# A one-layer diffusion step on one core: four modulation pieces ahead of the input projection instead of six, and their bias added on VectorE

## The chip, the core and the metric

The kernel runs on one NeuronCore of a Trainium2 chip. Its engines are PE (TensorE, matrix products), ACT (ScalarE), DVE (VectorE), POOL (GpSimd) and SP (SyncE, which here only issues DMAs). Time is device microseconds of one execution, and lower is better. Before the change three runs gave a median of 1856.68 us (1853.46 to 1857.34).

## What is computed

One layer over 640 tokens of width 1024: 128 context tokens (block 0) and 512 latent tokens (blocks 1 to 4). The part that the change touches:

```python
def modulation(cond, w_mod, b_mod):
    m = jax.nn.silu(cond) @ w_mod + b_mod          # (1024) @ (1024, 6144), for c and for c_ctx
    return jnp.split(m[..., None, :], 6, axis=-1)
...
sh1, sc1, g1, sh2, sc2, g2 = modulation(c, w_mod[l], b_mod[l])
h = rmsnorm(xs, norm1_g[l]) * (1 + sc1) + sh1
q, k, v, f = split_in(h, w_in[l])                  # h @ w_in, (1024, 2048)
...
xs = xs + g1 * mixer_merge(att, four, subln_g[l], lam_init, w_out[l])
h2 = rmsnorm(xs, norm2_g[l]) * (1 + sc2) + sh2
xs = xs + g2 * peer(h2, w_query[l], sub_keys[l], expert_u[l], expert_v[l])
```

Only shift 1 and scale 1 (the first third of the modulation) are needed by `h`, which the input projection takes; the rest is needed after the attention. Then follow rotary embedding, differential attention, a Fourier mix, an output projection, and a product-key retrieval over 16384 experts, in a loop of 64 passes that takes most of the time.

## The kernel before

Everything is float32. The kernel is written engine by engine in program order, with semaphores between engines; each engine runs its own list in order.

**Weights.** `w_mod` comes in 12 pieces of 1024x512 (2 MiB each, mod 0 to mod 11), `w_in` in four of the same size, which the code calls k, q, v and f by the heads that they give. All of them, then a table for the Fourier mix and two pieces of `w_out`, go through a ring of three slots of 2 MiB (`chunk`, `WRING = 3`). SP issues the loads in one order, `chunk_order()`: mod 0 to 5, k, mod 6, mod 7, q, mod 8, mod 9, v, mod 10, mod 11, f. Ahead of load i SP waits until piece i-3 has been used (L353). PE counts that in `s_chunk_used`: after the last product of a modulation piece, and after an input piece's last block (L1382, where PE first waits for its own last product and then runs a nop). SP is in order, so a load that has to wait holds back every later load.

**A modulation piece.** Both conditions at once: the 32-column array tiles hold (condition, half of the columns) in four groups of rows 0, 32, 64, 96, and PE runs 32 products of 256 columns (L1328), then four of one row times the bias (L1337), into one of eight PSUM banks. `mod_out(j)` on ACT copies row groups to `rows` (a ring of two, L557), and `spread_mod` on POOL broadcasts each of the four rows over 128 partitions (L451), into `M1` for mod 0 to 3 and into `M` or `G2` for the others.

**From the first four pieces to the projection.** DVE waits for 16 broadcasts (mod 0 to 3), turns scale 1 into (1 + scale) times the norm's weight (L873, two instructions of 1024 columns), and makes `H1` block by block in two instructions (L880, L882). PE transposes a block (L1354), ACT rounds it into `HT_hi` (L586), and DVE keeps the rest in `HT_lo` (L928). The piece of `w_in` is split in the same way, `w_hi` on ACT (L580, `weights_high`) and `w_lo` on DVE (L920, `weights_low`), each in eight steps. DVE's order is: three blocks of H1, `rows_low(0)`, half of `weights_low(0)`, `rows_low(1)`, the other half.

**The projection.** For each of k, q, v, f and each of five blocks PE runs 8 times three products of 512 columns (L1372, L1373, L1376); of block 0 each step waits for its `w_lo`. Blocks of k and q are rotated on DVE (L906 to L913), transposed back on PE (`headT`, L1389) and copied by ACT (L567). Between the input pieces PE computes the modulation pieces that `mods_ahead` names, two each time. I call the stretch from the last block of one input piece to the first product of the next a gap: gap 1 before q, gap 2 before v, gap 3 before f.

The order in which PE fills the eight banks is `_phase1_jobs()`; entry n needs that entry n-8 was emptied.

Of the kernel before, what the change touches and what calls it, by code (L numbers as in the profile page):

```python
# [20 lines left out]
MOD_FIRST = 6  # L21
# [30 lines left out]
def mods_ahead(ci):  # L52

    return [MOD_FIRST + 2 * (ci - 1) + w for w in range(2)]

# [10 lines left out]
def _phase1_jobs():  # L66
    jobs = [(("mod", j), "act") for j in range(MOD_FIRST)]
# [4 lines left out]
    for ci, (c, turned) in enumerate((("k", None), ("q", "k"), ("v", "q"), ("f", None))):  # L72
        if ci:
            jobs += [(("mod", j), "act") for j in mods_ahead(ci)]
# [52 lines left out]
def program(nc, xall, condT, w_mod, b_mod, norm1_g, w_in, lam4, subln_g, w_fourier, w_out, norm2_g,  # L127
# [7 lines left out]
    with ctx:  # L135
        def sb(name, shape, dt=f32):
            return ctx.enter_context(nc.sbuf_tensor(name, shape, dt))
# [5 lines left out]
        ones = sb("ones", [1, 32])  # L143
# [111 lines left out]
        bmod = cutout(CO, 6144, slice(0, 1))  # L255
        gbc = creg[:, 6144:8192].rearrange("p (w d) -> p w d", w=2)
        rows = creg[:, 8704:9216].rearrange("p (r n) -> p r n", r=2)
        bmod_late = cutout(XO + 4096, 1024, slice(0, 1))
# [31 lines left out]
        s_chunk_used = sem("s_chunk_used")  # L290
# [5 lines left out]
        s_rows = sem("s_rows"); s_bc = sem("s_bc")  # L296
# [36 lines left out]

        block = ctx.enter_context(nc.Block())
# [100 lines left out]
        def _(pool):  # L435
# [5 lines left out]
            def spread_mod(j):  # L441
                pool.wait_ge(s_rows, j + 1)
# [82 lines left out]
        def _(act):  # L525
            act.dma_start(cond[:, :, :], condT).then_inc(s_cond, 16)
            act.dma_start(bmod, b_mod).then_inc(s_bmod, 16)
# [7 lines left out]
            act.wait_ge(s_set, 1)  # L535
# [16 lines left out]

            def mod_out(j):
                src = bank1("mod", j)
                if j >= 2:
                    act.wait_ge(s_bc, 4 * (j - 1))
                act.copy(rows[:, j % 2, :], src[:, 0:HC]).then_inc(s_rows, 1)  # L557
                act.wait_ge(s_rows, j + 1)
                act.nop().then_inc(s_act1, 1)

            for j in range(MOD_FIRST):
                mod_out(j)

# [31 lines left out]
            def between(ci):  # L595

                mod_out(mods_ahead(ci)[0])
                weights_high(ci)
                mod_out(mods_ahead(ci)[1])

            for ci, c in enumerate(("k", "q")):
                if ci:
                    between(1)
                for b in range(NBLK):
# [8 lines left out]
                    else:  # L613
                        dst = kT if c == "k" else qT
# [8 lines left out]
            between(2)  # L623
            act.dma_start(bmod_late, b_mod[:, 10 * NC:12 * NC]).then_inc(s_bmod, 16)
# [9 lines left out]
            between(3)  # L634
# [206 lines left out]
        def _(dve):  # L841
# [11 lines left out]
            dve.memset(ones[:, :], 1.0).then_inc(s_set, 1)  # L853
# [15 lines left out]
            dve.tensor_scalar(ss[:, :], ss[:, :], 1.0 / D, EPS, ALU.mult, ALU.add).then_inc(s_var1, 1)  # L869
            dve.wait_ge(s_bc, 16)  # L870
# [12 lines left out]

            def bank1(*name):
                i = B1.pos[name]
                dve.wait_ge(s_fill1, i + 1)
                return ps[:, i % 8, :]
# [53 lines left out]
            for ci, c in enumerate(("k", "q")):  # L941
                for b in range(1, NBLK):
# [10 lines left out]
            dve.nop().then_inc(s_mod2, 1)  # L953
            weights_low(3)
            dve.tensor_copy(fold[:, 1], bank1("fold", 1).rearrange("p (g n) -> p g n", g=4)).then_inc(s_dve1, 1)
# [351 lines left out]
        def _(pe):  # L1307
# [12 lines left out]
            pe.wait_ge(s_set, 1)  # L1320
            pe.wait_ge(s_bmod, 16)
            def modulation(j):
# [3 lines left out]
                for k in range(KD):  # L1326
                    for q in range(4):
                        last = nc.tensor.matmul(out[32 * q:32 * q + 32, 0:HC], sil[:, k, q % 2, :],  # L1328
                                                chunk[:, i % WRING, k, q // 2 * HC:(q // 2 + 1) * HC],
                                                start=(k == 0), stop=False)  # L1330
                last.then_inc(s_chunk_used, 1)
                if j >= 8:
                    pe.wait_ge(s_bmod, 32 if j < 10 else 48)
                for q in range(4):
# [385 lines left out]
```

## Time and profile before

| what | value |
|---|---|
| median of 3 runs (lowest, highest) | 1856.68 us (1853.46, 1857.34) |
| span of the profiled execution | 1849.2 us |
| PE busy, of the span | 1726.7 us (93%) |
| DVE busy | 1498.4 us (81%) |
| POOL busy | 898.5 us (49%) |
| ACT busy | 678.4 us (37%) |
| HBM traffic over the span | 281 GB/s |
| modulation and projection (first product to last block of f) | 12 to 206 us |

The profiled execution's own time is given as its span alone, from its first instruction to its last, 7.5 us under the median of the runs. Busy shares are means over stages that have different limits: the expert loop, from about 440 us to the end, keeps PE, DVE and the DMA engines busy together, while the change lies in the first 206 us. There the question is at each point which of the engines or loads ended last.

### The profile page before, as it was taken

To read this page: it belongs to the slowest core of one execution; us is meant where nothing else is said; L and a number is where in the kernel's file an instruction comes from. 1 tells how busy PE (TensorE), PEld (TensorE's weight loads), DVE (VectorE), ACT (ScalarE), POOL (GpSimd) and SP (SyncE) were. 2 spreads that over 40 slices of the span, in tenths; PEclk is the share of its full clock that TensorE was granted. 3 is DMA by queue.
4 is the path that set the end of the run, shared out by engine and by line. 5 is a ranking of instruction groups with operands and counts; after the bars stand their busy time and mean duration, and the time that the engine had idled before them with its cause. 6 is when DMAs were issued, how large, how long until landed. Compare 5 with 4: busy or idle time off the path is not lost.

```text
span 1849.2 us, 29905 instructions
## 1 busy us (share of the span) xinstructions
PE 1726.7 (93%) x9942; PEld 1481.5 (80%) x9942; DVE 1498.4 (81%) x3027; ACT 678.4 (37%) x1135; POOL 898.5 (49%) x742
## 2 busy tenths in 40 slices
PE   4999998989899997699999999999999999999994
PEld 2677657448788886699999999999999999999993
DVE  0732057237888979899999999999999999999997
ACT  1212147010667763233333333333333333333332
POOL 1111001000242433488887878888666666666661
PEclk8999989999999998799999999999999999999997
DMA  9455101610055646899999999999999999999993
GB/s 355 163 186 223 62 1 42 243 46 1 2 110 114 134 101 183 314 402 399 405 401 392 403 407 407 403 404 401 407 405 396 403 407 399 398 405 407 402 397 138
DMA packets 253543, 520.91 MB, mean 282 GB/s; under 512 B 113955, under 2 KB 130979, under 8 KB 252197
## 3 DMA queue, kind: packets, MB, share of 16 engines
q1 hardware_dynamic: 178016, 249.00, 37.9%
q0 software_dynamic: 73728, 268.47, 36.7%
q10 hardware_dynamic: 1734, 2.60, 0.4%
q8 instruction: 38, 0.62, 0.1%
q14 instruction: 27, 0.22, 0.0%
HBM read 488.55 MB, written 31.46 MB: 281 GB/s over the span
## 4 chain that ended last, share of the span: by engine, by line
PE 57%; DVE 23%; issue 12%; DMA 5%; ACT 2%; DVEq 1%; SPq 0%; POOL 0%; POOLq 0%; PEldq 0%; ACTq 0%
DVE arena L1243 12%; PE ps L1626 9%; PE ps L1625 9%; PE ps L1624 9%; PE ps L1541 6%; PE ps L1522 4%; PE ps L1595 4%; DMA arena_w<-in_w_mod 2%; PE ps L1372 2%; PE ps L1376 2%; PE ps L1373 2%; PE ps L1459 2%; PE ps L1420 1%; DMA arena_w<-in_w_in 1%; DVE C_lo L1218 1%
## 5 line engine op out<-in xcount | busy, mean ns | idle before, releaser
L1624 PE MATMUL ps<-hT_hi,U_hi 128*128 128x384 f32 x1024 | 344.7, 337 | 11.7 <-DVE U_lo L1188 11.7
L1626 PE MATMUL ps<-hT_hi,U_lo 128*128 128x384 f32 x1024 | 344.7, 337 | 0.0
L1625 PE MATMUL ps<-hT_lo,U_hi 128*128 128x384 f32 x1024 | 344.0, 336 | 0.0
L1624 PE MATMUL ps<-V_hi,C_hi 128*128 128x512 f32 x768 | 300.1, 391 | 17.4 <-DVE C_lo L1218 17.4
L1626 PE MATMUL ps<-V_hi,C_lo 128*128 128x512 f32 x768 | 302.3, 394 | 0.0
L1625 PE MATMUL ps<-V_lo,C_hi 128*128 128x512 f32 x768 | 302.1, 393 | 0.0
L774 ACT CAST V_hi<-V_in 128x1024 fp32r<-128x1024 f32 x128 | 135.1, 1055 | 247.8 <-PE ps L1626 201.7
L480 POOL DMA_INDIRECT arena<-in_expert_u,idxn x128 | 173.4, 1355 | 81.3 <-issue 32.1
L811 ACT ACTIVATE act_t<-ps 128x384 f32<-128x384 f32 x128 | 63.0, 492 | 394.7 <-PE ps L1626 363.8
L1624 PEld LDWEIGHTS ps<-hT_hi,U_hi 128*128 128x128 f32 x1024 | 193.1, 189 | 16.8 <-issue 11.9
L480 POOL DMA_INDIRECT arena<-in_expert_v,idxn x128 | 159.0, 1243 | 93.3 <-DVE arena L1243 42.7
L1625 PEld LDWEIGHTS ps<-hT_lo,U_hi 128*128 128x128 f32 x1024 | 193.0, 189 | 4.9
L500 POOL TENSOR_SCALAR arena<-iota,arena 128x128 f32<-128x128 f32 x96 | 92.1, 970 | 208.7 <-PE ps L1595 128.9
L1626 PEld LDWEIGHTS ps<-hT_hi,U_lo 128*128 128x128 f32 x1024 | 192.9, 188 | 0.0
L1624 PEld LDWEIGHTS ps<-V_hi,C_hi 128*128 128x128 f32 x768 | 144.9, 189 | 45.5 <-DVE C_lo L1218 18.1
L1626 PEld LDWEIGHTS ps<-V_hi,C_lo 128*128 128x128 f32 x768 | 144.7, 188 | 30.7
L1243 DVE SCALAR_TENSOR_TENSOR arena<-arena,dots 128x1024 f32<-128x1024 f32 x128 | 165.0, 1289 | 4.7
L1625 PEld LDWEIGHTS ps<-V_lo,C_hi 128*128 128x128 f32 x768 | 144.8, 189 | 27.9
L1193 DVE TENSOR_TENSOR V_lo<-V_in,V_hi 128x1024 fp32r<-128x1024 f32 x128 | 156.5, 1223 | 12.9 <-ACT V_hi L774 11.5
L1188 DVE TENSOR_TENSOR U_lo<-U_in,U_hi 128x1024 fp32r<-128x1024 f32 x128 | 156.1, 1220 | 0.5 <-ACT U_hi L767 0.2
L1232 DVE SCALAR_TENSOR_TENSOR arena<-arena 128x1024 f32<-128x1024 f32 x128 | 153.7, 1220 | 3.0 <-DMA arena<-h_scratch 3.0
L767 ACT CAST U_hi<-U_in 128x1024 fp32r<-128x1024 f32 x128 | 134.0, 1047 | 34.0 <-DMA U_in<-in_expert_uT 31.6
(239 smaller groups left out, 3233.0 us busy)
## 6 DMA issues: line engine op xcount, KB each, us to landing
U_in<-in_expert_uT SPq DMA_DIRECT2D x128, 512.0 KB
V_in<-in_expert_v SPq DMA_DIRECT2D x128, 512.0 KB
arena_w<-in_w_mod SPq DMA_DIRECT2D x12, 2048.0 KB, 12.5
gates_scratch<-arena_w SPq DMA_DIRECT2D x6, 4096.0 KB, 20.8
gate_in<-gates_scratch SPq DMA_DIRECT2D x128, 192.0 KB
arena_w<-in_w_in SPq DMA_DIRECT2D x4, 2048.0 KB, 8.6
arena_w<-in_w_query SPq DMA_DIRECT2D x1, 7168.0 KB, 20.4
arena_w<-in_w_out SPq DMA_DIRECT2D x2, 2048.0 KB, 10.3
```

Of the source, the lines that this page charges most:

```text
L480: pool.indirect_dma_start(out=rowr[row], out_offset=None, in_=table, in_offset=bass.IndirectOffsetOnAxis(ap=idxn[:, g, row:row + 1], axis= ...
L500: ins = pool.tensor_scalar(rhs1[AIDED][:, t, :], iota[:, :], selT[:, b % 2, 0, at:at + 1], selT[:, b % 2, 1, at:at + 1], ALU.is_equal, ALU ...
L767: act.copy(U_hi[:, r], U_in[:, r]).then_inc(s_uhi, 1)
L774: act.copy(V_hi[:, r], V_in[:, r]).then_inc(s_vhi, 1)
L1188: dve.tensor_tensor(U_lo[:, r], U_in[:, r], U_hi[:, r].bitcast(f32), ALU.subtract).then_inc(s_ulo, 1)
L1193: dve.tensor_tensor(V_lo[:, r], V_in[:, r], V_hi[:, r].bitcast(f32), ALU.subtract).then_inc(s_vlo, 1)
L1232: dve.scalar_tensor_tensor(out=rowr[q], in0=rowr[q], scalar=1.0, in1=h2row[k], op0=ALU.mult, op1=ALU.mult, accum_out=dst).then_inc(s_used, 1)
L1243: dve.scalar_tensor_tensor(out=accS[:, k], in0=rowr[q], scalar=c, in1=accS[:, k], op0=ALU.mult, op1=ALU.add).then_inc(s_used, 1)
L1541: last = nc.tensor.matmul(out[:, j * P:(j + 1) * P], wq[:, k, c:c + P] if k < 7 else wq7[:, c:c + P], h2T[:, k, b * P:(b + 1) * P], start= ...
L1624: nc.tensor.matmul(out, hi, rhi, start=start, stop=False)
L1625: nc.tensor.matmul(out, hi, rlo, start=False, stop=False)
L1626: return nc.tensor.matmul(out, lo, rhi, start=False, stop=stop)
```

## The change

1. `MOD_FIRST` goes from 6 to 4, and `mods_ahead` gives three, three and two pieces to the gaps instead of two each. The order of loads becomes mod 0 to 3, k, mod 4, 5, 6, q, mod 7, 8, 9, v, mod 10, 11, f.
2. The bias is no longer four products on PE. It is loaded into rows 0, 32, 64 and 96 of two zeroed buffers, and `mod_out` is now one addition on DVE from the bank to `rows`.
3. `mod_out` stands on DVE: the first four after the variance of the input, and in each gap one ahead of `weights_low` and the others behind it. ACT's copies fall away.
4. SP waits on `s_fill1`, the count of filled banks, instead of `s_chunk_used`; PE's wait for itself and the nop fall away.
5. On ACT the four bias loads stand behind DVE's memset; the late bias waits for a second memset, on DVE behind the rotation of k's block 4. In q, ACT's copy of the first transposed block waits until mod 7 has been added, since the early bias lies where `qT` goes.

```diff
-MOD_FIRST = 6
+MOD_FIRST = 4
+MOD_EARLY = 8
...
 def mods_ahead(ci):
-    return [MOD_FIRST + 2 * (ci - 1) + w for w in range(2)]
+    return {1: [4, 5, 6], 2: [7, 8, 9], 3: [10, 11]}[ci]
...
-    jobs = [(("mod", j), "act") for j in range(MOD_FIRST)]
+    jobs = [(("mod", j), "dve") for j in range(MOD_FIRST)]
...
+        def bias_of(q, first, end):
+            return (b_mod.rearrange("o (j z n) -> o j z n", z=2, n=HC)[:, first:end, q // 2, :])
...
 # SP
                 if i >= WRING:
-                    sp.wait_ge(s_chunk_used, i - WRING + 1)
+                    kind, at = list(CHUNK)[i - WRING]
+                    sp.wait_ge(s_fill1, B1.pos[("mod", at) if kind == "mod" else ("z", "kqvf"[at], NBLK - 1)] + 1)
...
 # POOL
-                pool.wait_ge(s_rows, j + 1)
+                pool.wait_ge(s_dve1, B1.emptied(B1.pos["mod", j])[1])
...
 # ACT
-            act.dma_start(bmod, b_mod).then_inc(s_bmod, 16)
+            act.wait_ge(s_set, 1)
+            for q in range(4):
+                act.dma_start(bmod[32 * q:32 * q + 1], bias_of(q, 0, MOD_EARLY)).then_inc(s_bmod, 16)
...
-                mod_out(mods_ahead(ci)[0])
-                weights_high(ci)
-                mod_out(mods_ahead(ci)[1])
...
                     else:
+                        if ci and b == 1:
+                            act.wait_ge(s_dve1, B1.emptied(B1.pos["mod", MOD_EARLY - 1])[1])
...
                         if ci == 0 and b + 2 == NBLK:
-                            act.dma_start(bmod_late, b_mod[:, 8 * NC:10 * NC]).then_inc(s_bmod, 16)
+                            act.wait_ge(s_latefill, 1)
+                            for q in range(4):
+                                act.dma_start(bmod_late[32 * q:32 * q + 1], bias_of(q, MOD_EARLY, MOD_CH)).then_inc(s_bmod, 16)
...
 # DVE
-            dve.memset(ones[:, :], 1.0).then_inc(s_set, 1)
+            dve.memset(creg[:, 3072:3072 + MOD_EARLY * HC], 0.0).then_inc(s_set, 1)
...
+            def mod_out(j):
+                src = bank1("mod", j)
+                dve.wait_ge(s_bmod, 64 if j < MOD_EARLY else 128)
+                if j >= 2:
+                    dve.wait_ge(s_bc, 4 * (j - 1))
+                bias = bmod[:, j, :] if j < MOD_EARLY else bmod_late[:, j - MOD_EARLY, :]
+                dve.tensor_tensor(rows[:, j % 2, :], src[:, 0:HC], bias, ALU.add).then_inc(s_dve1, 1)
+            for j in range(MOD_FIRST):
+                mod_out(j)
             dve.wait_ge(s_bc, 16)
...
+                    if ci == 0 and b + 1 == NBLK:
+                        dve.wait_ge(s_fill1, B1.pos[("hT", NBLK - 1, 1)] + 1)
+                        dve.memset(cutout(XO + 4096, (MOD_CH - MOD_EARLY) * HC), 0.0).then_inc(s_latefill, 1)
+                mod_out(mods_ahead(ci + 1)[0])
                 weights_low(ci + 1)
+                for j in mods_ahead(ci + 1)[1:]:
+                    mod_out(j)
...
 # PE
-                last.then_inc(s_chunk_used, 1)
-                for q in range(4):
-                    at = q // 2 * HC
-                    bias = bmod[:, j * NC + at:j * NC + at + HC] if j < 8 else bmod_late[:, j % 2 * NC + at:j % 2 * NC + at + HC]
-                    last = nc.tensor.matmul(out[32 * q:32 * q + 32, 0:HC], ones[:, :], bias, start=False, stop=True)
                 last.then_inc(s_fill1, 1)
...
-                if b == NBLK - 1:
-                    pe.wait_ge(s_fill1, B1.pos[("z", c, b)] + 1)
-                    pe.nop().then_inc(s_chunk_used, 1)
```

SP, the loads from mod 0 to f (each 128x8x512 is one piece of 2 MiB; in_w_mod is modulation, in_w_in projection), before:

```order
L353 DMA arena_w<-in_w_mod 128x8x512
L341 DMA arena<-in_xall 128x5x1024
L353 DMA arena_w<-in_w_mod 128x8x512 x2
L353 DMA arena_w<-in_w_mod 128x8x512 [waits s_chunk_used] x3
L353 DMA arena_w<-in_w_in 128x8x512 [waits s_chunk_used]
L353 DMA arena_w<-in_w_mod 128x8x512 [waits s_chunk_used] x2
L353 DMA arena_w<-in_w_in 128x8x512 [waits s_chunk_used]
```

The same place of the changed kernel:

```order
L357 DMA arena_w<-in_w_mod 128x8x512
L344 DMA arena<-in_xall 128x5x1024
L357 DMA arena_w<-in_w_mod 128x8x512 x2
L357 DMA arena_w<-in_w_mod 128x8x512 [waits s_fill1]
L357 DMA arena_w<-in_w_in 128x8x512 [waits s_fill1]
L357 DMA arena_w<-in_w_mod 128x8x512 [waits s_fill1] x3
L357 DMA arena_w<-in_w_in 128x8x512 [waits s_fill1]
```

The load of k moved from seventh to fifth place, and three loads of modulation, not two, now stand between it and the load of q.

PE in gap 1 (L1389 is the last `headT` of k, L1328 and L1337 a modulation piece, L1372 q's first product; s_chunk0 to s_chunk2 are the slots of the ring), before:

```order
L1389 MATMUL ps<-ident,arena_w 128x128 [waits s_fill1,s_dve1]
L1389 MATMUL ps<-ident,arena_w 128x128 x3
L1328 MATMUL ps<-arena_w 32x256 [waits s_chunk1,s_dve1]
L1328 MATMUL ps<-arena_w 32x256 x31
L1337 MATMUL ps<-arena_w,ones 32x256 x4
L1328 MATMUL ps<-arena_w 32x256 [waits s_chunk2,s_act1]
L1372 MATMUL ps<-w_hi_next,HT_hi 128x512 [waits s_dve1,s_wlo,s_chunk0]
```

And in the changed kernel:

```order
L1386 MATMUL ps<-ident,arena_w 128x128 [waits s_dve1]
L1386 MATMUL ps<-ident,arena_w 128x128 x3
L1336 MATMUL ps<-arena_w 32x256 [waits s_chunk2,s_dve1]
L1336 MATMUL ps<-arena_w 32x256 x31
L1336 MATMUL ps<-arena_w 32x256 [waits s_chunk0,s_act1]
L1336 MATMUL ps<-arena_w 32x256 [waits s_chunk1,s_dve1]
L1373 MATMUL ps<-w_hi_next,HT_hi 128x512 [waits s_dve1,s_wlo,s_chunk2]
```

Three pieces stand here now. The third takes slot 1, where k lies until its last block, and q takes slot 2, where the first of the three lies.

DVE between the rotation of k's block 4 and that of q's block 1, before:

```order
L913 TENSOR_TENSOR arena_w<-arena_w 128x512 [waits s_step]
L920 TENSOR_TENSOR w_lo<-arena_w,w_hi_next 128x512 [waits s_whi] x8
L906 TENSOR_TENSOR arena_w<-ps,arena_w 128x512 [waits s_dve1,s_fill1]
```

And in the changed kernel:

```order
L914 TENSOR_TENSOR arena_w<-arena_w 128x512 [waits s_step]
L951 MEMSET arena 128x1024 [waits s_fill1]
L872 TENSOR_TENSOR arena_w<-ps,arena_w 128x256 [waits s_bc,s_bmod,s_fill1]
L921 TENSOR_TENSOR w_lo<-arena_w,w_hi_next 128x512 [waits s_whi] x8
L872 TENSOR_TENSOR arena_w<-ps,arena_w 128x256 [waits s_bc,s_bmod,s_fill1] x2
L907 TENSOR_TENSOR arena_w<-ps,arena_w 128x512 [waits s_dve1,s_fill1]
```

A memset and one addition now stand ahead of the split of q's weights, and two additions behind it.

## Rows read from the trace of the kernel before

**Rows 1.** The profile's page: the span, and the chain that ended last, by engine and by line.

```profile
span 1849.2 us, 29905 instructions
PE 57%; DVE 23%; issue 12%; DMA 5%; ACT 2%; DVEq 1%; SPq 0%; POOL 0%; POOLq 0%; PEldq 0%; ACTq 0%
DVE arena L1243 12%; PE ps L1626 9%; PE ps L1625 9%; PE ps L1624 9%; PE ps L1541 6%; PE ps L1522 4%; PE ps L1595 4%; DMA arena_w<-in_w_mod 2%; PE ps L1372 2%; PE ps L1376 2%; PE ps L1373 2%; PE ps L1459 2%; PE ps L1420 1%; DMA arena_w<-in_w_in 1%; DVE C_lo L1218 1%
```

**Rows 2.** The chain in order of time, front and gaps: start us, us, what.

```profile
37.54 12.53 DMA arena_w<-in_w_mod
50.11 3.66 PE ps L1328 x64
...
57.50 0.52 ACT w_hi_first L580
...
91.35 8.19 DMA arena_w<-in_w_in
99.56 0.63 ACT w_hi_next L580
...
101.05 0.47 PE ps L1372
...
130.56 8.02 DMA arena_w<-in_w_in
```

**Rows 3.** Timeline of DVE: start us, us, line, out<-in, count, [idle before <-releaser].

```profile
1.61 0.48 DVE L852 MEMSET arena_w<- 128x512 f32 x1
...
45.85 2.48 DVE L873 SCALAR_TENSOR_TENSOR arena_w<-arena_w 128x1024 f32<-128x1024 f32 x2 [18.52 <-POOL arena_w L451]
...
50.93 1.43 DVE L880 SCALAR_TENSOR_TENSOR arena<-arena,rstd,arena_w 128x1024 f32<-128x1024 f32 x1
...
55.09 1.32 DVE L882 TENSOR_TENSOR arena<-arena,arena_w 128x1024 f32<-128x1024 f32 x1
56.33 1.27 DVE L928 TENSOR_TENSOR HT_lo<-ps,HT_hi 128x512 fp32r<-128x512 f32 x2
58.04 2.50 DVE L920 TENSOR_TENSOR w_lo<-arena_w,w_hi_first 128x512 fp32r<-128x512 f32 x4 [0.43 <-ACT w_hi_first L580]
...
64.06 1.28 DVE L880 SCALAR_TENSOR_TENSOR arena<-arena,rstd,arena_w 128x1024 f32<-128x1024 f32 x1
```

**Rows 4.** Timeline of PE, front, gap 1, and after the attention.

```profile
42.88 0.63 PE L1337 MATMUL ps<-arena_w,ones 1*32 1x256 f32 x8
...
62.39 0.50 PE L1372 MATMUL ps<-w_hi_first,HT_hi 128*128 128x512 f32 x1 [0.54 <-DVE w_lo L920]
...
91.54 0.63 PE L1389 MATMUL ps<-ident,arena_w 128*128 128x128 f32 x4 [0.30 <-PE ps L1376]
...
324.21 1.12 PE L1492 MATMUL ps<-ident,arena_w 128*128 128x128 f32 x4 [4.58 <-DVE arena_w L998]
```

**Rows 5.** SP's loads of modulation in gaps 1 and 2, and their landing.

```profile
95.81 4.52 SPq L353 DMA_DIRECT2D arena_w<-in_w_mod  x2
...
DMA to landing us min/median/max: 11.4/11.4/11.4
...
135.02 4.52 SPq L353 DMA_DIRECT2D arena_w<-in_w_mod  x2
...
DMA to landing us min/median/max: 10.9/10.9/10.9
```

**Rows 6.** Two stretches: busy us of PE, PEld, DVE, ACT, POOL, PEclk, DMA, GB/s.

```profile
27.00:31.00 4.00, 4.00 (x48) 1.81 (x44) 0.17 (x1) 0.39 (x3) 1.18 (x1) 0.56 1.06 383
324.00:331.00 7.00, 6.01 (x10) 2.90 (x11) 0.16 (x1) 0.69 (x1) 0.00 (x0) 0.51 0.75 277
```

**Rows 7.** One shape of addition on DVE, one copy on ACT, PE's second modulation piece.

```profile
L909 DVE TENSOR_TENSOR arena_w<-ps,arena_w 128x256 f32<-128x256 f32 x16 | 6.0, 415 | 0.0
...
43.58 0.37 ACT L557 COPY arena_w<-ps 128x256 f32<-128x256 f32 x1 [5.10 <-PE ps L1337]
...
26.70 4.66 PE L1328 MATMUL ps<-arena_w 128*32 128x256 f32 x48 [8.12 <-DMA arena_w<-in_w_mod]
```

More of the change, by code:

```diff
@@ L73, in _phase1_jobs @@
         if ci:
-            jobs += [(("mod", j), "act") for j in mods_ahead(ci)]
+            jobs += [(("mod", j), "dve") for j in mods_ahead(ci)]
         for b in range(NBLK):
@@ L142, in program @@
         ident = sb("ident", [P, P])
-        ones = sb("ones", [1, 32])
         lam = sb("lam", [P, 8])
@@ L534, in _ @@
             act.wait_ge(s_cond, 16)
-            act.wait_ge(s_set, 1)
             act.activation(sig, cond[:, :, :], ACT.Exp, scale=-1.0).then_inc(s_exps, 1)
@@ L551, in bank1 @@
                 return ps[:, i % 8, :]
[L553 to L562, printed above, removed]
             def heads_out(name, dst):
@@ L593, in _ @@
             act.dma_start(V[:, 1, :], cache_v).then_inc(s_vc, 16)
-            def between(ci):
-                mod_out(mods_ahead(ci)[0])
-                weights_high(ci)
-                mod_out(mods_ahead(ci)[1])
             for ci, c in enumerate(("k", "q")):
                 if ci:
-                    between(1)
+                    weights_high(1)
                 for b in range(NBLK):
@@ L619, in _ @@
                         if ci == 0 and b + 2 == NBLK:
-                            act.dma_start(bmod_late, b_mod[:, 8 * NC:10 * NC]).then_inc(s_bmod, 16)
+                            act.wait_ge(s_latefill, 1)
+                            for q in range(4):
+                                act.dma_start(bmod_late[32 * q:32 * q + 1], bias_of(q, MOD_EARLY, MOD_CH)).then_inc(s_bmod, 16)
                     if b == 0 and ci:
                         heads_out(("headT", "k", NBLK - 1), kT[:, :, 5 * P:6 * P])
-            between(2)
-            act.dma_start(bmod_late, b_mod[:, 10 * NC:12 * NC]).then_inc(s_bmod, 16)
+            weights_high(2)
             for b in range(NBLK):
@@ L633, in _ @@
                     heads_out(("headT", "q", NBLK - 1), qT[:, :, 4 * P:5 * P])
-            between(3)
+            weights_high(3)
             for b in range(NBLK):
@@ L953, in _ @@
             dve.nop().then_inc(s_mod2, 1)
+            mod_out(mods_ahead(3)[0])
             weights_low(3)
+            for j in mods_ahead(3)[1:]:
+                mod_out(j)
             dve.tensor_copy(fold[:, 1], bank1("fold", 1).rearrange("p (g n) -> p g n", g=4)).then_inc(s_dve1, 1)
@@ L1329, in modulation @@
                                                 chunk[:, i % WRING, k, q // 2 * HC:(q // 2 + 1) * HC],
-                                                start=(k == 0), stop=False)
-                last.then_inc(s_chunk_used, 1)
-                if j >= 8:
-                    pe.wait_ge(s_bmod, 32 if j < 10 else 48)
-                for q in range(4):
-                    at = q // 2 * HC
-                    bias = bmod[:, j * NC + at:j * NC + at + HC] if j < 8 else bmod_late[:, j % 2 * NC + at:j % 2 * NC + at + HC]
-                    last = nc.tensor.matmul(out[32 * q:32 * q + 32, 0:HC], ones[:, :], bias, start=False, stop=True)
+                                                start=(k == 0), stop=(k == KD - 1))
                 last.then_inc(s_fill1, 1)
@@ L1439, in _ @@
             pe.wait_ge(s_fill1, B1.total)
-            pe.nop().then_inc(s_chunk_used, 1)
             pe.wait_ge(s_act1, B1.count("act"))
```

17 lines of the change are left out of this document (7 added, 10 removed).

## The prediction

> **What bounds the kernel now.** I read the page first, then the chain in order of time over the first 206 us, then the timelines of DVE, PE and SP there, and last the granted clock around PE's pauses. The page [rows 1] gives the span, 1849.2 us, and says that over the whole program modulation loads hold only 2% of the chain and projection loads 1%; the expert loop has the rest. The loop starts when the stages ahead of it are done and runs at its own rate, so a shift of its start passes to the end one to one. The stages in between are one string of PE work with nothing loaded late, so they pass a shift on too. The change is worth what it moves the first product of each of k, q, v and f.
>
> The chain there [rows 2] has two patterns. In the front it goes from a modulation load (landed at 37.54 + 12.53 = 50.07) to PE's sixth piece, then over ACT to w_hi at 57.50. In gaps 1 and 2 it goes from PE's last block to a projection load, issued at 91.35, landed at 99.54, first split step at 99.56, first product of q at 101.05; the next one is issued at 130.56 and lands at 138.58. The modulation pieces of the gap cost nothing there: they are multiplied while that load flies.
>
> But the chain shows only who came last. DVE [rows 3] begins L873 at 45.85, when the broadcasts of mod 3 end, and is then busy with H1 and HT_lo without a pause until it waits 0.43 us for w_hi and starts w_lo at 58.04. So DVE is late by nearly as much as the load: whatever leaves the front behind mod 3, k's first product cannot follow it further than DVE allows.
>
> **The front.** Mod 4 and 5 leave it, each a load of 2 MiB; at 383 GB/s [rows 6] that is 5.5 us each, 11.0 in all, and by the chain one would book that. DVE allows this:
> - Four bias products fall away. For mod 3 they are 0.63 us [rows 4], ahead of the copy, the broadcasts and L873. The copy is now an addition: 0.42 us on DVE (the same shape, L909) for 0.37 on ACT [rows 7], and ACT's nop goes. I take -0.6.
> - POOL no longer broadcasts mod 4 and 5 beside H1. L880 takes 1.43 us there and 1.28 later [rows 3]; two of them, -0.3.
> - The wait of 0.43 for w_hi goes, since the transposes no longer stand behind mod 5 on PE: -0.4.
> - So k starts at about 57.6 in place of 58.9. Its one stall of 0.54 [rows 4] goes too, as DVE leads by more: -0.5.
> - Against that, PE has almost nothing to do from 43 to 57.6. The trace shows what follows a pause: after 8.12 us of idle [rows 7] the granted clock is 0.56 over 27 to 31, that is mostly the lower level of 1.2 GHz, and 4.00 us of work there lose 4.00 x 0.44 = 1.8 us; after 4.58 us [rows 4] it is 0.51 over 324 to 331, and 6.01 busy us lose 2.9 [rows 6]. For k's start I take the row with the like pause, +1.8; bounds 0 and 2.9.
>
> The front's sum is -1.8 + 1.8 = 0.0, between -1.8 and +1.1. Next late there is DVE, then PE.
>
> The slower start is covered. DVE's memset is four times 0.48 us [rows 3], ACT's loads and its exponent come some 3 us later, but mod 0 was waiting for its load, and behind it PE idles 8.12 us for mod 1 [rows 7].
>
> **Gaps 1 and 2.** Call T the end of k's last block. Slot 1 is k's until T, so mod 6 can be issued only then, and SP, in order, issues q behind it; q also needs mod 4 done, which PE runs after T. So the projection load that was first behind T is now second, about 4.5 us later, with mod 7 third, behind mod 5. The trace has a load in exactly that place: in gap 1 SP issues modulation at 95.81 and 99.96 [rows 5], the first of these 4.46 us behind q, and it lands 11.4 us later, at 107.2. Put q there: 107.2 - 99.54 = +7.7. Gap 2: 135.02 + 10.9 = 145.9 against 138.58, +7.3. In both PE starts its first piece 0.3 us earlier, since its wait for its own product goes (the idle ahead of L1389 [rows 4]), so -0.3 each. Sum **+14.4**. Bounds: q lands 8.19 us behind its own issue as a first load does, which costs just the later issue, 4.46 - 0.3 = +4.2 a gap; or 12.53 behind it, as in the full queue of the front, 95.81 + 12.53 - 99.54 - 0.3 = +8.5 a gap [rows 2]. I take 11.4 and 10.9, the same place among the same neighbours.
>
> Why 11.4 when a load alone takes 8.2? By the row the second load ran beside the first until 99.5 and beside the third from about 101, and slowed with both. The Trainium skill, "DMA: Bandwidth & Descriptors", section on queues, rings and completion order, says that on each DMA engine the descriptors of one queue are consumed in ring order; by that a third load would not slow the second. It stands as a rival below.
>
> PE then waits. Mod 6 lands 8.2 us behind T, its products take 3.66 [rows 2], and q starts near T + 17: idle for 5.1 us. That lies by the pause of 4.58 us, which brought the lower clock [rows 4, 6]. q's products are paced by PE, so it loses 1.8 to 2.9 us; I take the mean, 2.3, in each gap: **+4.6**, bounds 0 and 5.8. The Trainium skill, "TensorE: Matmul & The Clock Gate", section on why this matters for your kernels, advises against pauses between bursts of matmuls for this reason; the sum above has it from the rows.
>
> Hidden in the gaps: DVE's memset of 1024 columns (twice 0.48) and one addition of 0.42 stand before q's w_lo, but that waits for q to land. The two additions behind w_lo stand ahead of a rotation which needs q's block 1. ACT, waiting for the late memset, holds back one headT copy; it has nothing else until q lands. In gap 2 ACT makes four copies that used to lie among q's blocks, after mod 7 is added, 4.5 us behind T; mod 8 waits about 1 us for a bank by it, but v lands at T + 15. Were v early instead, these would cost some 2 us. POOL's broadcasts of mod 4 to 11 are for uses far behind.
>
> **Gap 3** is as before: two pieces, both loaded ahead, and f is the first load behind v's last block.
>
> **Sum:** 0.0 + 14.4 + 4.6 = **+19.0 us**. The profiled execution would have a span of 1868.2. The median of the runs lies 7.5 above the span, so 1856.7 + 19.0 = **1875.7 us**, +1.0%. A measurement of this kernel can tell about 0.2%, 3.7 us, from no change.
>
> **The rivals.**
> - *The clock holds.* No product runs at 1.2 GHz, neither in the gaps nor in the front: 19.0 - 4.6 - 1.8 = +12.6, 1869.3. For it: only two pauses of this length are on record here, and neither follows a run of modulation products by 5 us. Against: both rows after pauses of over 4 us show the drop. Chance 0.13.
> - *Loads in strict order.* q lands one load behind mod 6, 99.5 + 5.5, a gap costs 5.5, the two 11.0, with the clock 15.6: 1872.3. Against it are the 11.4 and 10.9 us of [rows 5], 2 us later than this would give. Chance 0.13. This is the rule of the DMA page above.
> - *Everything late at once:* 12.5 us per second load and 2.9 of clock in all three places: 1.1 + 17.0 + 5.8 = +23.9, 1880.6. Chance 0.08.
> - *The front gives what the chain books.* k starts when its pieces are there: -11.0 for two loads, -0.6 for the bias, -0.3 for the broadcasts, -0.5 for the stall, and each gap costs only q's later issue, 4.2: -12.4 + 8.4 = -4.0, 1852.7, faster by 0.22%. It decides if DVE's work behind mod 3 can begin before 45.85 or be done in under 2 us. For it: the chain runs over DMA, PE and ACT in the front. Against it: L873 waited 18.52 us for POOL, which waits for mod 3, a load that keeps its place, and 11 us of DVE's instructions follow with no gap. Chance 0.03.
> - *The change does not act:* if SP's new waits were all met early, time would stay. The listing of SP's order shows the three loads between k and q, and the slots follow from that. Chance 0.02.
>
> **How the numbers follow.** The forecast has 0.61, and its own bounds are 1873 to 1878. The range reaches down past the held clock and up past the case with everything late: 1867 to 1882. Faster by over 0.2%: 0.03. Within 0.2%: 0.02. Slower by over 0.2%: 0.95.
>
> **What would show it.** L873 starts near 45.2 and k's first product near 57.5; if that were near 48, the front's reading is wrong. Behind T the first load is modulation and q is issued 4 us later, lands near T + 15.5, and q's first product is 7 us further from T than the 9.7 of before; the same in gap 2, while gap 3 stays as it was. The granted clock is below 1 at the start of k, q and v. From f's first product on both traces run alike. A gap near 14 us says strict order; a clock of 1.00 there says that rival. The prediction is wrong if the gaps are as long as before.

## The result, and the profile after

The changed kernel takes **1866.84 us** (median of 4 runs, 1864.51 to 1867.24), the kernel before 1856.08 (4 runs, 1853.46 to 1857.34). The ratio is 1.0059, 95% interval 1.0046 to 1.0071: slower by 10.8 us. The forecast was slower by 19.0. The sign and the place are right, the size is nearly twice too large; the result lies at the foot of the forecast's range (1867 to 1882, reckoned from a median before of 1856.68). Why is the subject of what follows.

The page of the changed kernel, as [rows 1]:

```profile
span 1862.4 us, 29705 instructions
PE 57%; DVE 21%; issue 12%; DMA 6%; ACT 2%; DVEq 1%; POOL 0%; ACTq 0%; SPq 0%; POOLq 0%
```

DMA's share of the chain went from 5 to 6%, and the span is 13.2 us longer. The chain in order of time, gaps 1, 2 and 3 (start us, us, what), beside [rows 2]:

```profile
89.94 3.63 PE ps L1336 x64
93.58 10.63 DMA arena_w<-in_w_in
104.24 0.62 ACT w_hi_next L573
104.89 0.70 DVE w_lo L921
105.73 0.47 PE ps L1373
...
139.22 11.36 DMA arena_w<-in_w_in
...
181.67 8.14 DMA arena_w<-in_w_in
```

In [rows 2] q's load was issued at 91.35, as soon as k's last block was done, and landed 8.19 us later. Now PE first multiplies mod 4 (L1336, 3.63 us), only then q's load goes out, and it takes 10.63 us; v's takes 11.36. In gap 3 f's load takes 8.14 us. In the kernel before it took longer, which [rows 2] don't show:

```profile
168.16 9.11 DMA arena_w<-in_w_in
```

DVE in the front (start us, us, line, out<-in, count, idle before), beside [rows 3]:

```profile
42.06 0.42 DVE L872 TENSOR_TENSOR arena_w<-ps,arena_w 128x256 f32<-128x256 f32 x1 [5.00 <-PE ps L1336]
44.38 2.48 DVE L879 SCALAR_TENSOR_TENSOR arena_w<-arena_w 128x1024 f32<-128x1024 f32 x2 [1.90 <-POOL arena_w L455]
...
54.27 1.28 DVE L929 TENSOR_TENSOR HT_lo<-ps,HT_hi 128x512 fp32r<-128x512 f32 x2
55.47 2.48 DVE L921 TENSOR_TENSOR w_lo<-arena_w,w_hi_first 128x512 fp32r<-128x512 f32 x4
```

DVE turns the scale 1.5 us earlier than in [rows 3] (44.38 for 45.85; the line is now L879) and is then busy up to `w_lo` without a wait. PE's waits (the same columns), beside [rows 4]:

```profile
38.33 3.66 PE L1336 MATMUL ps<-arena_w 128*32 128x256 f32 x64 [1.76 <-DMA arena_w<-in_w_mod]
...
49.50 1.97 PE L1355 MATMUL ps<-ident,arena 128*128 128x128 f32 x8 [6.92 <-DVE arena L888]
...
56.30 0.47 PE L1373 MATMUL ps<-w_hi_first,HT_hi 128*128 128x512 f32 x1 [2.63 <-DVE w_lo L921]
...
98.97 3.66 PE L1336 MATMUL ps<-arena_w 128*32 128x256 f32 x64 [1.99 <-DMA arena_w<-in_w_mod]
105.73 0.47 PE L1373 MATMUL ps<-w_hi_next,HT_hi 128*128 128x512 f32 x1 [3.10 <-DVE w_lo L921]
...
140.33 7.11 PE L1336 MATMUL ps<-arena_w 128*32 128x256 f32 x128 [1.18 <-ACT arena_w L560]
152.08 0.62 PE L1373 MATMUL ps<-w_hi_next,HT_hi 128*128 128x512 f32 x1 [4.64 <-DVE w_lo L921]
```

SP's issues in gap 1 (start us, us, queue, line, out<-in, count), modulation first and q's piece second, where [rows 5] have the second place taken by modulation:

```profile
89.53 0.37 SPq L357 DMA_DIRECT2D arena_w<-in_w_mod  x1
93.58 0.37 SPq L357 DMA_DIRECT2D arena_w<-in_w_in  x1
```

The granted clock at the starts of k, q, v and f (columns as in [rows 6]: busy us of PE, PEld, DVE, ACT, POOL, PEclk, DMA, GB/s):

```profile
57.00:61.00 4.00, 4.00 (x13) 3.14 (x12) 4.00 (x8) 1.44 (x3) 0.00 (x0) 0.61 0.00 0
105.00:110.00 5.00, 4.27 (x19) 3.58 (x20) 5.00 (x9) 3.50 (x7) 0.00 (x0) 1.00 1.04 387
152.00:157.00 5.00, 4.92 (x15) 3.94 (x16) 4.81 (x9) 2.85 (x6) 0.43 (x2) 0.66 1.05 389
191.00:196.00 5.00, 4.67 (x21) 3.90 (x22) 4.72 (x9) 3.10 (x6) 0.19 (x1) 1.00 0.98 404
```

The clock is partly at the lower level at the starts of k and v, and at the full one at those of q and f. The next table is from PE's timelines of both kernels, in us. An input piece runs from the start of its first product to the end of its last one:

| | before | after | moved |
|---|---|---|---|
| k starts | 58.88 | 56.30 | -2.58 |
| k runs | 32.19 | 33.03 | +0.84 |
| gap 1 | 9.98 | 16.40 | +6.42 |
| q runs | 29.23 | 29.23 | 0.00 |
| gap 2 | 9.81 | 17.12 | +7.31 |
| v runs | 27.79 | 29.40 | +1.61 |
| gap 3 | 10.90 | 9.85 | -1.05 |
| f runs | 27.29 | 27.30 | +0.01 |
| f's last product ends | 206.07 | 218.63 | +12.56 |

Nearly everything happens up to f's last product: 12.56 of the span's 13.2 us.

### The profile page after: what moved, and what is told of

Read it like the earlier page. It is cut to its first block, busy times and chain, and to the rows that moved or that the text cites. A ratio compares the mean times of both kernels' runs of the same rounds, so it can differ in the third digit from the quotient of the medians.

```text
span 1862.4 us, 29705 instructions
## 1 busy us (share of the span) xinstructions
PE 1724.7 (93%) x9846; PEld 1485.0 (80%) x9846; DVE 1504.1 (81%) x3040; ACT 677.1 (36%) x1123; POOL 892.9 (48%) x742
## 4 chain that ended last, share of the span: by engine, by line
PE 57%; DVE 21%; issue 12%; DMA 6%; ACT 2%; DVEq 1%; POOL 0%; ACTq 0%; SPq 0%; POOLq 0%
PE ps L1622 9%; PE ps L1621 9%; PE ps L1620 9%; DVE arena L1253 9%; PE ps L1537 6%; PE ps L1518 4%; PE ps L1591 4%; DMA U_in<-in_expert_uT 3%; DVE V_lo L1203 3%; PE ps L1373 2%; PE ps L1377 2%; PE ps L1374 2%; DMA arena_w<-in_w_in 2%; PE ps L1455 2%; PE ps L1417 1%
## 5 line engine op out<-in xcount | busy, mean ns | idle before, releaser
L484 POOL DMA_INDIRECT arena<-in_expert_u,idxn x128 | 168.2, 1314 | 81.3 <-issue 32.1
```

What stands on the lines that cost most here:

```text
L484: pool.indirect_dma_start(out=rowr[row], out_offset=None, in_=table, in_offset=bass.IndirectOffsetOnAxis(ap=idxn[:, g, row:row + 1], axis= ...
```

## The experiments

Each ratio is against runs of the kernel before that were made beside the experiment: 17 for e1 to e4 (median 1855.04 us), 22 for e4b, e6, e7 and e8 (1855.3), 15 for e9 (1854.63), 10 for e9b (1854.46) and 15 for e10 (1855.33). `arena_w` is the buffer region that holds the loads, `bank1(...)` the PSUM bank of a named result.

### One half of the change at a time

**e1_bias_dve**: pieces as before (6, 2, 2, 2), bias added on DVE.

```diff
-MOD_FIRST = 4
+MOD_FIRST = 6
...
-    return {1: [4, 5, 6], 2: [7, 8, 9], 3: [10, 11]}[ci]
+    return [MOD_FIRST + 2 * (ci - 1) + w for w in range(2)]
...
-            for j in range(MOD_FIRST):
+            for j in range(4):
...
+            for j in range(4, MOD_FIRST):
+                mod_out(j)
```

> The changed kernel with the pieces placed as before (six first, then two in each gap); the bias on DVE stays, and mod 4 and 5 are added behind the third block of H1. If the place of the pieces costs the time, nothing of the +10.8 us is left: between -3 and 0 us against the kernel before, from mod 3 being broadcast 1 to 1.5 us sooner and PE's wait for its own product gone. If the additions on DVE or the later loads on ACT cost it, +5 us or more stays.

**e2_order_only**: the kernel before with four pieces first and three, three and two in the gaps, bias still on PE.

```diff
-MOD_FIRST = 6
+MOD_FIRST = 4
...
-    return [MOD_FIRST + 2 * (ci - 1) + w for w in range(2)]
+    return {1: [4, 5, 6], 2: [7, 8, 9], 3: [10, 11]}[ci]
...
+        bmod_mid = cutout(MO + 3072, 2048, slice(0, 1))
...
```

> The kernel before with the pieces placed as in the change (4, 3, 3, 2), bias still as products on PE and copies on ACT. If the place of the pieces is the cause: +11 to +16 us against before, a little more than the change itself, since each piece keeps its 0.63 us of bias products and the front is not helped. If DVE's additions are the cause: within 3 us of before.

Measured: e1 1854.4 us, ratio 0.9997 (0.9988 to 1.0006); e2 1869.66 us, ratio 1.0071 (1.0058 to 1.0084). The bias on DVE alone is worth nothing that can be measured, and the order alone brings the whole loss. Gaps 1, 2 and 3 are 11.35, 9.56 and 9.89 us in e1 and 16.73, 16.14 and 11.39 in e2. That e2 is above the changed kernel, by ratio 0.0012 with overlapping intervals, leaves open whether the bias gives something back in the new order.

### What makes the second load late

**e3_hold**: the changed kernel, but SP holds the load behind a projection load until that one has landed. If the load behind q takes bandwidth from q, this must shorten the gap. The table of the Fourier stage is held behind f in the same way.

```diff
+                if 0 < i < DFT_C and list(CHUNK)[i - 1][0] == "in":
+                    sp.wait_ge(s_chunk[(i - 1) % WRING], 16 * ((i - 1) // WRING + 1))
...
+                    sp.wait_ge(s_chunk[i % WRING], 16 * (i // WRING + 1))
```

> The changed kernel, but SP issues no further load until the projection piece in flight (k, q, v, f) has landed. If loads in flight share the DMA engines: q and v land about 9 us behind their issue instead of 10.6 and 11.4, f 1 us sooner or at the same time, together -3 to -5 us against the changed kernel, so +6 to +8 against before. If loads of one queue are served in order: q and v land as now, +10.8 against before within 1 us.

Measured: 1868.85 us, ratio 1.0071 (1.0056 to 1.0086). The chain of e3_hold in order of time, and in the second fence SP's issues in gap 1:

```profile
93.81 10.33 DMA arena_w<-in_w_in
...
140.49 10.50 DMA arena_w<-in_w_in
```

```profile
93.81 0.37 SPq L359 DMA_DIRECT2D arena_w<-in_w_in  x1
104.16 32.64 SPq L359 DMA_DIRECT2D arena_w<-in_w_mod  x3
```

The third load now goes out at 104.16, when q has landed, and q still takes 10.33 us in place of 10.63, v 10.50 in place of 11.36. The gaps are 16.10, 16.27 and 9.93 us, so 0.3 and 0.9 us came back where sharing would have given some 2 us each, and in the whole time nothing did. My reason in the prediction falls as the main one. Whether the third load costs v anything isn't settled: e7_five below has it and lands v after 10.71.

What is left is the load ahead. In gap 1 of the changed kernel q lands 5.4 us behind mod 6 (mod 6 was there at 98.8, q at 104.2), which is one load of 2 MiB at 383 GB/s [rows 6]. That looks as if the queue handed over one load after the other. The Trainium skill, "DMA: Bandwidth & Descriptors", section on queues, rings and completion order, states that each DMA engine takes the descriptors of a ring in order; the two landings in gap 1 agree with it. As a price it is too low in general: in gap 2 v lands 7.5 us behind mod 9 (143.1 and 150.6), in gap 2 of e3_hold it is 6.5 us, and in the kernel before the second loads of [rows 5] land 7.7 and 7.3 us behind the first. Counted from the issue of the first load the second is steadier: 14.3 to 15.9 us in all of these gaps, where it is issued 4.0 to 4.5 us behind the first. Why it is more than one load's time stays open.

**e7_five**: five pieces first, two behind k, three behind q. Gap 1 has q's load first again, gap 2 has v's load second.

```diff
-MOD_FIRST = 4
+MOD_FIRST = 5
...
-    return {1: [4, 5, 6], 2: [7, 8, 9], 3: [10, 11]}[ci]
+    return {1: [5, 6], 2: [7, 8, 9], 3: [10, 11]}[ci]
...
```

> The changed kernel with five pieces first, then two, three and two. Now k's load has q's load as the third behind it and takes its slot, so behind k's last block q is issued first; behind q's last block a modulation piece still is. If the place of the projection load in the queue decides: gap 1 about 9.8 us, gap 2 about 16 to 17, gap 3 about 10, +5 to +8 against before. If the number of pieces behind the first ones decides, each costing alike, also about half; but if three pieces in a gap were harmless and something in the front costs, +9 or more.

Measured: 1858.5 us, ratio 1.0023 (1.0014 to 1.0032). Its gaps are 10.02, 16.47 and 9.74 us. The chain of e7_five:

```profile
90.50 8.31 DMA arena_w<-in_w_in
...
133.80 10.71 DMA arena_w<-in_w_in
```

Only the gap in which a modulation load goes ahead of the projection load is long, and it is long by the same 6 to 7 us. The loss follows the place in the queue, not the number of pieces in the gap.

**e8_q_first**: the changed kernel with q, v and f each loaded first behind the last block, and the pieces that no longer fit multiplied behind the first blocks of q, v and f.

```diff
+WITHIN = {("q", 0): 6, ("v", 0): 8, ("v", 1): 9, ("f", 0): 10, ("f", 1): 11}
...
+    order = [("mod", j) for j in range(MOD_FIRST)] + [("in", 0), ("mod", 4), ("mod", 5), ("in", 1), ("mod", 6), ("mod", 7),
+             ("in", 2), ("mod", 8), ("mod", 9), ("in", 3), ("mod", 10), ("mod", 11)]
...
```

> The changed kernel with the loads in another order: k, mod 4, mod 5, q, mod 6, mod 7, v, mod 8, mod 9, f, mod 10, mod 11, so that behind each last block the projection load is issued first; mod 6 is multiplied behind q's block 0, mod 8 and 9 behind v's blocks 0 and 1, mod 10 and 11 behind f's. If q's place in the queue makes gap 1 16.4 us: it is 9.8 here, gap 2 and 3 about 9.8 too, and q's stage is 3.7 us longer, v's and f's 7.3. If DVE's additions, the memset or the late bias on ACT make it: gap 1 stays at 13 us or more. The table of the Fourier mix now waits for f's last block, so behind f some 11 us are lost, and the whole is slower than the changed kernel.

Measured: 1887.42 us in its single run, so without an interval. PE's timeline of e8_q_first at the start of the Fourier stage:

```profile
237.53 3.63 PE L1409 MATMUL ps<-arena_w 128*128 128x512 f32 x4 [8.50 <-issue]
```

q's load has the first place behind k again and lands after 9.09 us by the chain.

The gaps are 10.80, 9.62 and 9.90 us, so the place in the queue is confirmed a second time; but as a cure it fails. The pieces now cost 3.7 to 4.1 us each inside q, v and f, where nothing hides them. With fewer pieces in the gaps PE pauses for 5.42 us before v and 9.74 before f, and the granted clock is 0.52 over 144 to 149 and 0.50 over 191 to 196.5. The table for the Fourier stage, loaded last, leaves PE idle for 8.50 us behind f.

### What the clock takes

**e4_warm** and **e4b_warm**: the changed kernel with filler products of the identity in PE's pauses in the front, gap 1 and gap 2, written into the bank that is filled next. Shown is e4b; e4 has about twice as many in each pause.

```diff
+            def warm(out, count):
+                for _ in range(count):
+                    nc.tensor.matmul(out[:, 0:P], ident[:, :], ident[:, :], start=True, stop=True)
...
+            warm(bank1("hT", 0, 0), 29)
+            warm(bank1("hT", 1, 0), 3)
+            warm(bank1("z", "k", 0), 10)
...
+                if ci in (1, 2):
+                    warm(bank1("z", c, 0), {1: 11, 2: 17}[ci])
```

> The changed kernel with PE kept busy in its pauses by small products of ident with itself (58, 10 and 28 in the front, 12 and 22 in gap 1, 34 in gap 2), into banks that are filled next. If the granted clock costs what the trace shows (about 1.7 us at k's start, 1.6 at v's, none at q's in the profiled execution): clock 1.00 there and -2 to -5 us against the changed kernel, +6 to +9 against before. If products of this size do not hold the clock, or it costs nothing: +10 to +12.

> The changed kernel with PE's pauses filled again, with half as many products (29, 3 and 10 in the front, 7 and 11 in gap 1, 17 in gap 2), since one of them takes 0.223 us (58 took 12.95) and not 0.11. If the granted clock costs what the stages show (k's stage 1.4 us longer than with the clock up, v's 1.6, q's 0 to 2.8 by the execution): k and v as short as in the overfilled run (31.4 and 27.8), no stage longer, and -2 to -5 us against the changed kernel, +6 to +9 against before. If filling costs as much as it gives: +10 to +12.

e4_warm took 1877.95 us, ratio 1.0118 (1.0103 to 1.0132). PE's timeline of e4_warm:

```profile
41.86 13.12 PE L1362 MATMUL ps<-ident 128*128 128x128 f32 x116
```

58 fillers take 13.12 us, 0.226 each and not half of that (each shows as two passes), so they overran the pause of 6.92 us and pushed the work behind them. With half as many, e4b_warm took 1861.87 us, ratio 1.0034 (1.0021 to 1.0046), against 1.0059 of the changed kernel: 0.0025 of 1855 us, 4.6 us gained, or 1 to 8 with both intervals. The clock of e4b_warm, same columns as above:

```profile
56.00:60.00 4.00, 3.45 (x14) 2.59 (x15) 4.00 (x8) 1.54 (x3) 0.00 (x0) 1.00 0.00 0
104.50:109.00 4.50, 4.41 (x19) 3.67 (x20) 4.50 (x9) 2.87 (x6) 0.00 (x0) 1.00 1.04 386
150.60:155.00 4.40, 4.36 (x19) 3.64 (x20) 4.40 (x9) 2.82 (x6) 0.00 (x0) 1.00 1.03 380
```

The clock stays at its higher level at all three starts, with gaps as long as in the changed kernel (16.36, 16.79, 9.93 us). So by the medians the clock at these starts is worth nearly half of the changed kernel's loss. Not all of that need be the change's doing: the kernel before loses clock at the start of k or f in some executions too, as e10's trace shows below.

### The front

**e6_late_loads**: the kernel before, with ACT's small loads held back by a longer memset, as the changed kernel holds them back.

```diff
-            dve.memset(ones[:, :], 1.0).then_inc(s_set, 1)
+            dve.memset(ones[:, :], 1.0)
+            dve.memset(creg[:, 9216:11264], 0.0).then_inc(s_set, 1)
...
+            act.wait_ge(s_set, 1)
             act.dma_start(bmod, b_mod).then_inc(s_bmod, 16)
```

> The kernel before, where ACT issues its eight small loads behind a memset of 2048 columns on DVE, at 4.4 us instead of 1.2, as the change does. If that is why mod 3 landed 1 us sooner in the changed kernel (the DMA engines moved 164 GB/s from 8 to 10 us before and 405 after): the dip is gone, mod 5 lands about 1 us sooner, and k's first product too, 0 to -1.5 us against before. If the earlier landing had another cause: 39.3 us as before for mod 3, no difference.

Measured: 1853.42 us, ratio 0.9994 (0.9985 to 1.0003). The first large loads in the kernel before, and then in e6_late_loads:

```profile
8.00:10.00 2.00, 0.00 (x0) 0.00 (x0) 0.00 (x0) 0.00 (x0) 0.00 (x0) 1.00 0.59 164
```

```profile
8.00:10.00 2.00, 0.00 (x0) 0.00 (x0) 0.61 (x3) 1.23 (x2) 0.00 (x0) 1.00 1.02 389
```

While ACT's small loads run beside mod 0, the kernel before moves 164 GB/s; held back, it moves 389. The string of six loads then runs 0.65 us ahead (mod 3's products at 38.64 for 39.29, k's first product at 58.24 for 58.88). That is the same shift, in part, that the changed kernel has at mod 3 (38.33). In the whole time it can't be told from none.

### A version that beats both

**e9_warm_later**, **e9b_free_bank** and **e10_fill_only** are the kernel before, with its own order, and with fillers in the two pauses behind the attention, of which the first is in [rows 4, 6] (4.58 us idle, then 0.51 over 324 to 331). e9 and e9b have e6's late loads too, e10 has not. e9 puts the last 28 fillers into the bank of the third `h2T` block, e9b and e10 into a bank that is free.

```diff
+                if b == NBLK - 1:
+                    pe.wait_ge(s_exp, 2 * len(UNITS))
+                    warm(ps[:, 0, :], 17)
                 pe.wait_ge(s_att, b + 1)
...
+            warm(ps[:, 0, :], 3)
             pe.wait_ge(s_mix, NBLK)
...
+                if b == 2:
+                    warm(ps[:, 4, :], 28)
                 pe.wait_ge(s_h2, b + 1)
```

> The kernel before with its small loads delayed (as in e6_late_loads, 1853.42 us) and filler products of 0.223 us each in the two later pauses of PE that the profile shows with a low clock behind them: 17 ahead of the last attT and 3 ahead of the merge (pause 4.58 us, then 6.01 busy us at 0.51, a loss of 2.9 us), and 28 ahead of the third h2T block (pause 6.99 us, then 0.84 over 407 to 414 with 6.02 busy us, a loss of about 1.0). If the loss behind a pause is what the prediction took it for, a time that reaches the expert loop, the granted clock reads 1.00 over 324 to 331 and over 407 to 414 and the time falls by 3.9 us to about 1849.5. If the fillers end after the transposes become ready, the time stays near 1853.4. If the rest of those stages is paced by DVE or by loads, the clock rises and the time doesn't move.

> e9_warm_later with its 28 later fillers in a bank that nobody waits for. There they sat in the bank of the third h2T block and waited for ACT's copy at 406, so that they ran at half the clock behind the pause, 9.12 us, and pushed the transposes from 406.3 to 415.0; the first 20 fillers held the clock at 1.00 and won 2.5 us up to the end of the merge (from 8.3 us behind to 397.26 against 397.41 in e6_late_loads, with the first projections done 2.4 us later). If the fillers fit in the pause (28 of 0.223 are 6.2 us in 6.99), the transposes start at 406 with the clock at 1.00 over 407 to 414 and the time is 2.5 + 1.0 us under e6_late_loads' 1853.4: 1849.9. If only the earlier pause pays, 1850.9. If the expert loop doesn't take the gain, 1853.4.

> The kernel before with the 48 fillers of e9b_free_bank and nothing else, so without the delayed small loads. e9b_free_bank took 1848.7 us beside 1854.46 of before (ratio 0.9968), e6_late_loads, which has the delayed loads alone, 1853.42 beside 1855.3 (0.9994). If the two parts add up, this one has a ratio of 0.9974, some 1850 us, and nearly all the gain is the clock behind the two pauses. If the delayed loads carry a part that e6_late_loads' own interval hid, it stays above 0.9985.

| | median us | ratio | interval |
|---|---|---|---|
| e9_warm_later | 1858.21 | 1.0021 | 1.0012 to 1.0030 |
| e9b_free_bank | 1848.70 | 0.9968 | 0.9956 to 0.9980 |
| e10_fill_only | 1851.50 | 0.9978 | 0.9969 to 0.9987 |

PE's timeline of e9_warm_later:

```profile
406.07 9.12 PE L1491 MATMUL ps<-ident 128*128 128x128 f32 x56 [6.90 <-ACT arena L734]
415.04 2.78 PE L1543 MATMUL ps<-ident,arena_w 128*128 128x128 f32 x24
```

The 28 fillers wait for ACT to empty their bank, run behind the pause instead of in it, partly at the lower level of the clock, and cost 8.7 us of path. In the free bank they fill it (e9b_free_bank, PE's timeline):

```profile
400.32 6.42 PE L1491 MATMUL ps<-ident 128*128 128x128 f32 x56
407.49 3.02 PE L1543 MATMUL ps<-ident,arena_w 128*128 128x128 f32 x24 [0.75 <-ACT arena L734]
```

The chains show what either pause gave in the profiled executions. e6_late_loads comes first, then e9b_free_bank:

```profile
326.54 71.04 PE ps L1523 x160
...
406.31 2.81 PE ps L1532 x12
409.14 0.59 ACT arena L734
409.74 1.57 ACT arena L734 x3
411.31 0.25 issue
411.56 7.40 PE ps L1542 x64
```

```profile
329.81 68.95 PE ps L1532 x160
...
406.76 5.00 ACT arena L734 x10
411.76 0.24 issue
412.01 7.40 PE ps L1553 x64
```

The merge takes 68.95 us in place of 71.04, in e10's trace too. The stretch behind the second pause takes 5.25 us in both (406.31 to 411.56, 406.76 to 412.01): with a fast PE, ACT's ten copies set it. So in these executions the 20 fillers before the merge gave 2.1 us and the 28 later ones nothing. Between the medians e10 gains 3.8 us and e9b 5.8. Where the rest comes from isn't shown: no run has the 20 fillers alone, and another execution of the kernel before may lose more behind either pause than the one in the trace. e10 says that fillers alone give 0.9978; e9b's 0.9968 overlaps with it, so what the late loads add isn't settled.

## Why the prediction was right or wrong

By its own steps, from the profiled execution. The forecast of each step is on record above; the right column is what the table of milestones shows.

| step | forecast | measured |
|---|---|---|
| front, with the clock in k | 0.0 | -1.74 |
| gap 1, place in the queue | +7.4 | +6.42 |
| clock behind gap 1 | +2.3 | 0.00 |
| gap 2, place in the queue | +7.0 | +7.31 |
| clock behind gap 2 | +2.3 | +1.61 |
| gap 3 | 0.0 | -1.05 |
| behind f | 0.0 | +0.6 |
| sum | +19.0 | +13.2 |

**Right: the front isn't worth what its chain says.** Two loads of 5.5 us left the chain and k moved by 2.6 us, because DVE's work behind mod 3 stays: k's first product waits for its `w_lo`. L879 (then L873) began at 44.38 where 45.2 was forecast, k at 56.30 where 57.6 was. Of the missing 1.3 us 0.8 lie ahead of L879: mod 3's products began at 38.33 for 39.29, which the prediction had costed at nothing. The edit behind it is that ACT's small loads start later, and e6 shows that this alone gives 0.65 us there. Another 0.4 lie in DVE's stretch behind it, 11.09 us from L879 to `w_lo` for the 11.46 that [rows 3] give once the wait and the slower L880 are taken off: without POOL beside them, L888's additions too took 1.22 us in place of 1.32.

**Right: the two gaps and what makes them long.** The projection load is second behind the last block and is issued 4 us later; gap 3 stays within 1.1 us. e7 and e8 moved the place in the queue and the gap went with it. The size, +13.7 for a forecast of +14.4, rests on [rows 5], and holds.

**Wrong: the reason for the 11.4 us.** I took the second load to be slowed by the third and gave strict order 0.13, with 5.5 a gap. e3 took the third load away and won 0.3 us in gap 1 and 0.9 in v's landing. In gap 1 the second load lands one load's time behind the first, which is the rival's mechanism; but the first one took 9.3 us (89.5 to 98.8), not 8.2, so the gap cost 6.4 and not 5.5. In gap 2 the first took 7.9 us and the second landed 7.5 behind it, so there the rival's price was too low by itself. That the sum for the gaps came near is due to [rows 5], which hold whatever makes a second load late, and not to the reason that I gave.

**Not in the prediction: instruction loads.** The traces show what goes with the slow first loads. Packets of 16 KB, which the profile calls instruction, run on the same DMA engines. In the changed kernel one starts 3.9 us behind mod 6's issue, in the kernel before one starts 6.1 us behind f's. The DMA view of the changed kernel over 93 to 95 us, then that of the kernel before over 173 to 176 (packets, MB, share of 16 engines):

```profile
q8 instruction: 1, 0.02, 3.2%
```

```profile
q8 instruction: 1, 0.02, 2.3%
```

These shares are some 1.0 and 1.1 us of one engine. The 13 kept traces have 39 loads of 2 MiB that go out first behind the last block of k, q or v. The 14 with such a packet 3.4 to 6.8 us behind their issue took 8.7 to 9.6 us; the other 25, some with a packet in their last 1.1 us, took 7.8 to 8.3. (The bounds 3.4 and 6.8 are read off these same loads.) That a load has landed only when its slowest engine is done would explain it: in e3_hold, where q flies alone at the end, the mean busy share of the 16 engines is 0.07 from 103 to 104 us, about one of them, and q lands at 104.1. No run was made to test it. It accounts for the 1.1 us of mod 6 and for gap 3: f's load took 9.11 us before and 8.14 after, with no such packet beside it, and the gap is 1.05 us shorter.

**Wrong: the clock.** I took each pause of 4 to 5 us to cost 2.3 us, from two rows. In the profiled execution the pause of 3.10 us before q cost nothing and that of 4.64 before v 1.6. It isn't a function of the pause alone: in e1_bias_dve a pause of 3.70 us before q is followed by

```profile
101.40:106.00 4.60, 4.57 (x11) 3.63 (x12) 4.42 (x8) 2.80 (x6) 0.09 (x1) 0.50 1.04 389
```

and q runs 32.06 us in place of 29.23, a loss of 2.8. Even the short pause before f, where the kernel before stood 2.06 us and kept its clock, can cost as much. e10_fill_only is the same program up to there, and its trace has

```profile
179.27 0.77 PE L1372 MATMUL ps<-w_hi_next,HT_hi 128*128 128x512 f32 x1 [2.36 <-DVE w_lo L920]
```

```profile
179.00:184.00 5.00, 4.73 (x11) 3.80 (x12) 4.34 (x8) 3.31 (x7) 1.60 (x2) 0.50 0.97 387
```

with f running 30.12 us in place of 27.29. So the term is a chance between 0 and 2.8 us per start, the starts of the kernel before included, and one profile shows one draw. e4b puts it by the medians at some 4.6 us for the three places; I had 6.4 with the front, the profiled execution lost about 3. The Trainium skill, "TensorE: Matmul & The Clock Gate", Part 1, says that how many products run cold varies from run to run of one kernel; the rows agree.

**Wrong: the median's distance to the span.** I set it to 7.5 us, from the three times and the one span of before. A run's time is only 1.8 to 2.1 us above its own span in the four runs of the changed kernel, and 1.8 to 1.9 in 79 of the kernel before. The rest was that the profiled execution of before was a fast one: with 1.8 us added its span gives 1851.0, under all four runs that stand beside it. Its mean clock is 0.975, and of the 79 runs of that kernel in the experiments the two at 0.975 have a median of 1850.4, the 27 at 0.971 one of 1855.9, the five at 0.970 1856.2. The profiled execution of the changed kernel is nearer to its median (0.972 for 0.967 and 0.968 in the other three). So 13.2 us between two profiles are 10.8 between medians. That accounts for 2.4 of the 8.2 us of error, the clock in the gaps for 3.0, the front for 1.7, the three gaps together for 1.7, less 0.6 behind f.

The rival "the clock holds" gave 1869.3 and is nearest to the result, for the wrong reason: the clock did fall, only less, and the front and gap 3 gave the rest.

## What to carry to other kernels

When a step is moved ahead of a load in a queue, find the load's place behind the moment at which its slot comes free: first place landed in 7.8 to 9.6 us here, second in 9.9 to 11.4 behind an issue that is itself 4 us later, with or without a third behind it. A chain that runs over loads in the front books all of them as path; before counting on one, look whether another engine (here DVE) ends within 2 us of it. Read the clock behind a pause over several executions before it becomes a term of the sum, and if PE idles for 4 us ahead of PE-paced work, put as many products as fit in the pause into a bank that nobody waits for.

## What was not expected of the hardware

- The mean clock of an execution goes with its time: over 79 runs of one unchanged kernel, 0.970 to 0.975 goes with 1856.2 to 1850.4 us.
- A first load of 2 MiB took 8.7 to 9.6 us when a 16 KB instruction packet came 3.4 to 6.8 us behind its issue (14 loads), and 7.8 to 8.3 us otherwise (25 loads).
- ACT's small loads beside the first large one cut the rate to 164 GB/s over 2 us; held back, 389.
- A product of 128x128 in fp32 against the identity takes 0.226 us, in two passes, as 13.12 us for 58 show; with 20 of them in a pause of 4.58 us the merge behind it takes 68.95 us in place of 71.04.
